# Last expert's rows placed by TensorE, x loaded and turned first, constants on SP's queue, key blocks reordered

## The chip, the cores and the metric
One core of one Trainium2 chip. The metric is the device time in microseconds of one execution, over several runs of each kernel.

## The reference
One layer of a diffusion backbone on 128 context tokens (condition c_ctx) and 512 latent tokens (condition c), width 1024, all in f32:

```
sh1, sc1, gt1, sh2, sc2, gt2 = silu(cond) @ w_ada + b_ada
h = rms_norm(x) * g_pre * (1 + sc1) + sh1 ;  p = h @ w_in
A: 8 heads, 2 kv heads, normed q/k, all latent keys and 128 cached keys
B: 8 heads, 2 kv heads, window of +-128, 128 cached keys, a sink logit
x = x + gt1 * rms_norm(concat(A, B) @ w_out) * g_post
h = modulate(x, sh2, sc2); aff = softmax(h @ w_router); 16 experts take their top 64 (latent), 16 (context) tokens
y_e = (silu(h_e @ w_gate) * (h_e @ w_up)) @ w_down * g ; summed onto the tokens
out = x + gt2 * rms_norm(sum) * g_post_ffn
```
Context tokens attend to context tokens only. The keys and values of the context are outputs too.

## The kernel before, in words
Tokens lie in TILES = 5 tiles of 128 (tile 0 context, 1 to 4 latent). Each engine has its own instruction stream; order is set by hand with semaphores. SP issues the large loads in the order of UNITS (the loop at L334): units of 2 MB into six slots of a ring, first ada(0) and ada(1) (w_ada's columns for shift and scale, two units each, 4 KB rows), the five tiles of x ahead of unit 2, the first unit of w_in (keys and values, two DMAs of 1 KB rows), its second unit, and then w_ada units whose slots come free when ada(0) and ada(1) are done.

Start. ACT issues six early loads (identity, gains, b_ada spread onto 32 rows a quarter: L801 to L806) and 17 loads of constants through `load` (L797). After them it computes silu of the condition (L826), the squares of x (L830) and, with the root from POOL, x normalised (L833). PE runs ada(0), turns its columns (mod_columns, L448), turns two of eight column blocks of x (turn_x, L464), runs ada(1), and then in project(0) turns a block, has it modulated by DVE (L1062) and ACT (L839) on the way out of PSUM, and multiplies the block before (L485). project(i) goes through 3 units of w_in times 5 tiles; ada(2) to ada(5) lie between (ADA_AFTER: ada(2) after project(2)). turn_qk (L502) turns the split q and k. POOL zeroes the DRAM sums sum_l, sum_c after project(0) (L1425).

Attention. 80 units (group, head, tile); group A first. Per unit u PE turns the probabilities of u - 1 (L546), computes the scores of u + 2 (L534), and every second unit multiplies with the values (L568). DVE takes the maximum (L1190) and scales (L1258), ACT does exp (L910) and copies the turned probabilities (L953). Cached keys lie at key columns 0 to 127, latent ones behind. key_parts gives the score matmuls of a unit: A 512 and 128 columns, B the cached keys and the window; each part is done twice (high and low part of the key). In B, w_out is multiplied beside it (L615).

Experts. Per expert 12 MB of weights pass through the ring; product_l (L721) and product_c (L733) use four column groups of PE at a time. turn_rows(e + 1) (L699, L701) turns the gathered rows of the next expert. DVE's weigh (L1376, L1377) scales the result, POOL's loop adds it in DRAM with two indirect DMAs (L1475, L1477).

End. When the last scatter has landed, SP reads the sums (L411), ACT squares them (L1013), DVE and POOL form mean and root and gate them (L1389, L1391, L1485), DVE adds x1 (L1399), ACT issues the stores (L1018).

## Time and profile before

| | us |
|---|---|
| median of 3 runs | 1024.57 (1022.05 to 1025.99) |
| the profiled execution, its own time | 1026.47 |
| its span | 1024.6 |
| PE busy | 911.5 (89%) |
| DVE, ACT, POOL busy | 335.3, 208.5, 138.9 |
| DMA | 269.03 MB, 263 GB/s mean |
| mean granted TensorE clock | 0.956 |

PE, PEld, DVE, ACT, POOL and SP are the engines, PE's weight loads being PEld; SPq, ACTq and POOLq rows are issues of DMAs. A matmul in f32 leaves two records. The span runs from the first to the last instruction or transfer.

### The profile page before, as it was taken

The page shows a single profiled execution, that of the slowest core. Times are in us where ns is not written, and L with a number is a line of the kernel's source. Part 1 is how long each engine was busy: PE and PEld are TensorE (multiplying, and loading weights), DVE is VectorE, ACT ScalarE, POOL GpSimd, SP SyncE. Part 2 cuts the span into 40 slices and gives each one's busy share as a digit, 9 for nine tenths or more (in the row PEclk, how much of TensorE's full clock was granted, in tenths as well). Part 3 has the DMA queues.
Part 4 walks back from the last instruction along what each step waited for, and adds up shares of the span by engine and source line. Part 5 has one row for each costly group of instructions (what it writes and reads, how often), then busy time and mean ns, then how long its engine had stood idle before and what let it go on. Part 6 is the DMA issues. An engine that isn't in the chain of part 4 may idle for free.

```text
span 1024.6 us, 20086 instructions
## 1 busy us (share of the span) xinstructions
PE 911.5 (89%) x8615; PEld 458.3 (45%) x8615; DVE 335.3 (33%) x880; ACT 208.5 (20%) x487; POOL 138.9 (14%) x213
## 2 busy tenths in 40 slices
PE   0399999899999999648999999999999999999970
PEld 0145555477776655443444444444444443444420
DVE  0045453587786774461011101111011100111015
ACT  0412221366664543030000000000000000000002
POOL 0110110000000000012022210222022210222034
PEclk9989999989999999668999999999999999999995
DMA  9976630220000004956999999999999999999735
GB/s 316 366 271 230 243 143 26 94 107 2 1 2 1 21 21 150 370 214 218 382 383 393 393 410 394 393 394 397 406 393 393 393 410 393 393 393 395 290 99 212
DMA packets 79101, 269.03 MB, mean 263 GB/s; under 512 B 6512, under 2 KB 13040, under 8 KB 79056
## 3 DMA queue, kind: packets, MB, share of 16 engines
q1 hardware_dynamic: 64816, 244.99, 61.6%
q0 software_dynamic: 7632, 16.13, 6.3%
q10 hardware_dynamic: 6608, 7.29, 2.1%
q8 instruction: 31, 0.51, 0.2%
q14 instruction: 14, 0.11, 0.0%
HBM read 253.84 MB, written 14.55 MB: 262 GB/s over the span
## 4 chain that ended last, share of the span: by engine, by line
PE 52%; DVE 2%; DMA 1%; issue 1%; ACT 1%; DVEq 0%; POOL 0%; SPq 0%; POOLq 0%; ACTq 0%
PE ps L721 32%; PE ps L733 17%; PE ps L699 1%; PE ps L767 1%; PE ps L762 1%; DMA reg_qt<-sum_l 0%; DMA sum_c<-reg,kt 0%; DVE reg_qt L1391 0%; PE ps L701 0%; PE ps L638 0%; DVE reg_qt L1399 0%; DMA reg<-rows_c,kt 0%; ACT reg L983 0%; DVE kt L1302 0%; DVEq L106 0%
## 5 line engine op out<-in xcount | busy, mean ns | idle before, releaser
L721 PE MATMUL ps<-ring,reg 128*32 128x512 f32 x2048 | 231.4, 592 | 0.0
L733 PE MATMUL ps<-ring,reg 128*32 128x256 f32 x2048 | 124.2, 384 | 3.2 <-DVE reg L1361 2.2
L721 PEld LDWEIGHTS ps<-ring,reg 128*32 128x32 f32 x2048 | 66.5, 110 | 126.2 <-issue 115.2
L1376 DVE TENSOR_SCALAR reg<-ps,kt 128x512 f32<-128x512 f32 x16 | 12.0, 751 | 330.3 <-PE ps L721 330.3
L485 PE MATMUL ps<-ring,reg_qt 128*128 128x512 f32 x240 | 106.5, 594 | 0.0
L733 PEld LDWEIGHTS ps<-ring,reg 128*32 128x32 f32 x2048 | 65.1, 111 | 68.6 <-issue 31.6
L1000 ACT ACTIVATE reg<-ps 128x256 f32<-128x256 f32 x16 | 6.1, 383 | 405.1 <-PE ps L762 405.1
L1419 POOL TENSOR_TENSOR small<-small,mhalf 128x1 f32<-128x1 f32 (+2 forms) x30 | 26.2, 876 | 396.2 <-DVE small L1208 246.1
L615 PE MATMUL ps<-ring,reg 128*128 128x512 f32 x160 | 78.6, 621 | 0.0
L485 PEld LDWEIGHTS ps<-ring,reg_qt 128*128 128x128 f32 x240 | 44.1, 190 | 50.0 <-issue 50.0
L437 PE MATMUL ps<-ring,reg 128*32 128x256 f32 x384 | 27.0, 444 | 41.0 <-ACT reg L826 41.0
L953 ACT ACTIVATE ring<-ps 128x640 f32<-128x640 f32 (+3 forms) x80 | 44.3, 553 | 71.5 <-PE ps L546 69.3
L721 PE MATMUL ps<-reg_qt,kt 128*32 128x512 f32 x512 | 57.9, 592 | 0.0
L721 PE MATMUL ps<-ring,kt 128*32 128x512 f32 x512 | 57.9, 592 | 0.0
L1190 DVE TENSOR_REDUCE small<-ps 128x1 f32<-128x640 f32 (+3 forms) x80 | 50.9, 636 | 15.0 <-PE ps L534 13.8
L546 PE MATMUL ps<-ident,ring 128*128 128x128 f32 x288 | 47.8, 284 | 6.1 <-ACT ring L953 4.0
L1446 POOL TENSOR_TENSOR small<-mhalf 128x1 f32<-128x1 f32 x34 | 6.5, 191 | 336.6 <-DVE reg L1377 335.1
L910 ACT ACTIVATE ring<-ps,small 128x640 f32<-128x640 f32 (+3 forms) x80 | 50.9, 636 | 0.7 <-DVE small L1195 0.7
L546 PEld LDWEIGHTS ps<-ident,ring 128*128 128x128 f32 x288 | 33.1, 142 | 28.5 <-issue 18.4
L615 PEld LDWEIGHTS ps<-ring,reg 128*128 128x128 f32 x160 | 29.0, 196 | 26.2 <-issue 26.2
L1258 DVE TENSOR_SCALAR ring<-ring,small 128x640 f32<-128x640 f32 (+3 forms) x80 | 36.8, 460 | 2.8
L437 PEld LDWEIGHTS ps<-ring,reg 128*32 128x32 f32 x384 | 13.5, 127 | 52.7 <-ACT reg L826 41.0
(177 smaller groups left out, 983.6 us busy)
## 6 DMA issues: line engine op xcount, KB each, us to landing
ring<-in_w_up SPq DMA_DIRECT2D x32, 2048.0 KB, 17.4
ring<-in_w_down SPq DMA_DIRECT2D x32, 2048.0 KB
ring<-in_w_gate SPq DMA_DIRECT2D x16, 2048.0 KB, 14.8
reg_qt<-in_w_gate SPq DMA_DIRECT2D x16, 2048.0 KB, 15.6
ring<-in_w_ada SPq DMA_DIRECT2D x12, 2048.0 KB, 10.9
reg<-in_x_sample SPq DMA_DIRECT2D x8, 512.0 KB, 13.6
ring<-in_w_in SPq DMA_DIRECT2D x2, 2048.0 KB, 17.0
ring<-in_w_out SPq DMA_DIRECT2D x2, 2048.0 KB
```

Source lines behind the costliest of these rows:

```text
L437: last = pe.matmul(ps[32 * q:32 * q + 32, 4, 0:QUART], silu[:, 4 * h + c, :], w[:, c, q * QUART:(q + 1) * QUART], start=(h == 0 and c == 0 ...
L485: last = pe.matmul(ps[:, i % 2, :], hT[:, c, t * P:(t + 1) * P], w[:, c, :], start=(c == 0), stop=(c == KC - 1))
L546: last = pe.transpose(two[2][:, b * P:(b + 1) * P], probs[:, u % 3, b * P:(b + 1) * P], ident[:, :])
L615: last = pe.matmul(out_at(o)[:, n, :], attnT[:, c, t * P:(t + 1) * P], unit_at(wout_units[c // 4], 4)[:, c % 4, n * 512:(n + 1) * 512], st ...
L721: last = pe.matmul(o[64 * n + r:64 * n + r + 32, :], x[:, j, hf, r:r + 32], w[:, j, n * HALF:(n + 1) * HALF], start=(hf == 0 and j == 0), ...
L733: last = pe.matmul(o[32 * q:32 * q + 32, :], x[:, c % 2, c // 2, :], w[:, j, q * QUART:(q + 1) * QUART], start=(c == 0), stop=(c == KC - 1))
L910: act.activation(probs[:, u % 3, 0:n], scores_at(u)[:, 0:n], ACT.Exp, bias=negm[:, b:b + 1], scale=DH ** -0.5, accum_out=den[:, b:b + 1]). ...
L953: act.activation(pT[:, k % 2, u % 2, 0:n], two[2][:, 0:n], ACT.Copy).then_inc(pT_ready, 1)
L1190: link(dve.tensor_reduce(mx[:, b:b + 1], scores_at(u)[:, 0:n], AX.X, ALU.max))
L1258: dve.tensor_scalar(probs[:, u % 3, 0:n], probs[:, u % 3, 0:n], rden[:, b:b + 1], None, ALU.mult)\
L1376: dve.tensor_scalar(y_l, ps[:, 3, :], g_l[:, bass.ds(e, 1)], None, ALU.mult)
L1419: pool.tensor_tensor(dst, mean, mhalf[:, 0:n], ALU.pow).then_inc(done, 1)
```

## The change
- Start: x is loaded ahead of all weights; b_ada goes to the two used rows of each quarter of a buffer that DVE has cleared. The constants are issued by SP, seven of them (keys, gains, rope) behind the first w_in unit and waited for as keys_in, ten behind the second as consts_in. The first w_in unit comes in two halves of K. PE turns all eight blocks of x before ada(0); they are copied out unmodulated and modulated in place afterwards.
- Attention: the cached keys lie between latent blocks 1 and 2, so that a window is one stretch of columns. A's scores are 320 + 320 columns, B's one part.
- Last expert: no turn_rows, no weigh, no scatter. POOL numbers the columns, DVE builds from them matrices that hold the gate at (row, its token) and PE multiplies them with the copied result: context sums and tile 1 are added to the loaded sums by DVE, for tiles 2 to 4 PE adds the loaded sum with an identity matmul. Squares and gating read PSUM. SP waits for the sums of the other 15 experts, reads them, and issues the stores. POOL gathers no rows past the last expert.

```diff
...
-POOL_GATED = (0, 2)
+SUM_BANKS = {1: 6, 2: 0, 3: 2, 4: 4}
+SUMMED_BY_PE = (2, 3, 4)
...
+KEY_AT = {-1: 2 * P, 0: 0, 1: P, 2: 3 * P, 3: 4 * P}
+WINDOWS = {1: [0, 1, -1], 2: [0, 1, -1, 2], 3: [1, -1, 2, 3], 4: [-1, 2, 3]}
...
+def value_blocks(g, t):
+    if t == 0:
+        return [4]
+    return [0, 1, -1, 2, 3] if g == 0 else WINDOWS[t]
...
 def key_parts(g, t):
     if t == 0:
         return [(0, TOK, CTX)]
+    first, n = KEY_AT[value_blocks(g, t)[0]], key_count(g, t)
     if g == 0:
-        return [(0, 0, 512), (512, 512, TOK - 512)]
-    lo, hi = max(0, t - 2), min(LT - 1, t)
-    return [(0, 0, CTX), (CTX, CTX + lo * P, (hi + 1 - lo) * P)]
...
+        return [(0, first, n // 2), (512, first + n // 2, n // 2)]
+    return [(0, first, n)]
...
+            def load_keys():
+                for n, name in enumerate(("cache_a_k", "cache_a_v", "cache_b_k", "cache_b_v")):
+                    sp.dma_start(cache[:, n * P:(n + 1) * P], A[name][0, 0].rearrange("t h d -> t (h d)")).then_inc(keys_in, 16)
+                for n, name in enumerate(("g_qa", "g_ka")):
+                    sp.dma_start(gqk[:, n * DH:(n + 1) * DH], A[name].to_broadcast([P, DH])).then_inc(keys_in, 16)
+                sp.dma_start(rope[:, :, :, :].rearrange("p a t d -> p (a t) d"),
+                             A["rope_tables"].rearrange("a (t p) d -> p (a t) d", p=P)).then_inc(keys_in, 16)
+            def load_consts():
+                sp.dma_start(sink[:, :], A["sink_b"].to_broadcast([P, HEADS])).then_inc(consts_in, 16)
+                sp.dma_start(wr[:, :].rearrange("p (c e) -> p c e", e=E),
+                             A["w_router"][0].rearrange("(c p) e -> p c e", p=P)).then_inc(consts_in, 16)
+                for n, name in enumerate(("g_post_attn", "g_post_ffn")):
+                    rows = A[name].rearrange("a (q n) -> q a n", q=4)
+                    for q in range(4):
+                        sp.dma_start(gpost[32 * q:32 * q + 32, n * QUART:(n + 1) * QUART],
+                                     rows[q].to_broadcast([32, QUART])).then_inc(consts_in, 16)
...
-                if u == 2:
+                if u == 0:
...
                     if m == 0:
-                        sp.dma_start(d[:, :, 0:256], w[:, :, 512:768]).then_inc(slot_in[slot_of(u)], 16)
-                        sp.dma_start(d[:, :, 256:512], w[:, :, 1280:1536]).then_inc(slot_in[slot_of(u)], 16)
+                        for b in (0, 1):
+                            k = slice(4 * b, 4 * b + 4)
+                            sp.dma_start(d[:, k, 0:256], w[:, k, 512:768]).then_inc(win0_in[b], 16)
+                            sp.dma_start(d[:, k, 256:512], w[:, k, 1280:1536]).then_inc(win0_in[b], 16)
+                        load_keys()
...
+                        if m == 1:
+                            load_consts()
...
-            sp.wait_ge(added_l, 16 * (E + 1))
-            sp.wait_ge(added_c, 16 * (E + 1))
+            sp.wait_ge(added_l, 16 * E)
+            sp.wait_ge(added_c, 16 * E)
+            sp.wait_ge(gate_b, E)
...
+            for t in range(TILES):
+                sp.wait_ge(f_ready, t + 1)
+                dst = out[0][0] if t == 0 else out[1][0, (t - 1) * P:t * P]
+                sp.dma_start(dst, gated[:, t, :]).then_inc(stored, 16)
+            sp.wait_ge(stored, 16 * (4 + TILES))
...
-            pe.wait_ge(silu_ready, 1)
-            ada(0)
             pe.wait_ge(early_in, 16 * N_EARLY)
-            mod_columns(0, 0)
...
-                    pe.wait_ge(ht_ready, c - 1)
-                    pe.wait_ge(htc_ready, c - 1)
+                    pe.wait_ge(ht_raw, c - 1)
+                    pe.wait_ge(htc_raw, c - 1)
...
-            turn_x(0)
-            turn_x(1)
+            for c in range(KC):
+                turn_x(c)
+            pe.wait_ge(silu_ready, 1)
+            ada(0)
+            mod_columns(0, 0)
             ada(1)
             mod_columns(1, 1)
...
                 for c in range(KC):
                     if i == 0:
-                        if c + 2 < KC:
-                            turn_x(c + 2)
                         pe.wait_ge(htc_ready, c + 1)
+                        if c % 4 == 0:
+                            pe.wait_ge(win0_in[c // 4], 32)
...
-                turn_rows(e + 1)
+                if not final:
+                    turn_rows(e + 1)
...
+                if final:
+                    weight_in(5, e)
+                    product_c(5, YC[:, 0:QUART], aT_c).then_inc(down_c, 1)
+                    pe.wait_ge(actT_l_ready, e + 1)
+                    product_l(4, Y, aT_l).then_inc(down_a, 1)
+                    product_l(5, Y, aT_l).then_inc(down_b, 1)
+                    return
...
+            def total_onto(t, n):
+                pe.wait_ge(sum_in[t], 16)
+                pe.matmul(sums_at(t)[:, n, :], ident[:, :], total[:, t, n * HALF:(n + 1) * HALF], start=True, stop=False)
+            def last_onto(t):
+                for n in (0, 1):
+                    last = pe.matmul(sums_at(t)[:, n, :], put_on_l[64 * n:64 * n + 64, (t - 1) * P:t * P],
+                                     y_l[64 * n:64 * n + 64, :], start=t not in SUMMED_BY_PE, stop=True)
+                last.then_inc(put_on, 1)
+            pe.wait_ge(put_on_ready, 1)
+            pe.wait_ge(y_copied_c, 1)
+            pe.wait_ge(silu_done, 2 * E)
+            pe.wait_ge(actT_l_ready, E)
+            for q in range(4):
+                last = pe.matmul(ps[:, (0, 1, 2, 5)[q], 0:QUART], put_on_c[32 * q:32 * q + 32, :],
+                                 y_c[32 * q:32 * q + 32, :], start=True, stop=True)
+            last.then_inc(put_on, 1)
+            pe.wait_ge(f_added, 1)
+            total_onto(2, 0)
+            pe.wait_ge(y_copied_l, 1)
+            last_onto(1)
+            total_onto(2, 1)
+            last_onto(2)
+            for t in (3, 4):
+                total_onto(t, 0)
+                total_onto(t, 1)
+                last_onto(t)
...
+            act.wait_ge(bias_cleared, 1)
             for q in range(4):
-                act.dma_start(modq[32 * q:32 * q + 32, :, :], b_rows[q:q + 1].to_broadcast([32, N_MOD, QUART]))\
+                act.dma_start(modq[32 * q:32 * q + 2, :, :], b_rows[q:q + 1].to_broadcast([2, N_MOD, QUART]))\
...
+            for c in range(KC):
+                act.wait_ge(xt_done, c + 1)
+                act.activation(hT[:, c, 0:P], ps[:, 5 + c % 2, 0:P], ACT.Copy).then_inc(htc_raw, 1)
...
             act.wait_ge(modcol_ready, 2)
             for c in range(KC):
-                act.wait_ge(xt_done, c + 1)
-                act.activation(hT[:, c, 0:P], ps[:, 5 + c % 2, 0:P], ACT.Identity, bias=cmod[:, 0, 0, c:c + 1],
+                act.wait_ge(htc_raw, c + 1)
+                act.activation(hT[:, c, 0:P], hT[:, c, 0:P], ACT.Identity, bias=cmod[:, 0, 0, c:c + 1],
                                scale=cmod[:, 1, 0, c:c + 1]).then_inc(htc_ready, 1)
...
-                    act.wait_ge(consts_in, 16 * N_CONSTS)
+                    act.wait_ge(keys_in, 16 * N_KEYS)
...
-                act.activation(probs[:, u % 3, 0:n], scores_at(u)[:, 0:n], ACT.Exp, bias=negm[:, b:b + 1],
+                dst = probs[:, u % 3, 0:n]
+                if g == 0 and t:
+                    dst = dst.rearrange("p (b n) -> p b n", b=2)
+                act.activation(dst, scores_of(u), ACT.Exp, bias=negm[:, b:b + 1],
                                scale=DH ** -0.5, accum_out=den[:, b:b + 1]).then_inc(exp_done, 1)
...
-            for t in range(TILES):
-                act.wait_ge(sum_in[t], 16)
-                act.activation(squares[:, t, :], total[:, t, :], ACT.Square,
+            act.wait_ge(added_l, 16 * E)
+            act.wait_ge(added_c, 16 * E)
+            act.wait_ge(down_c, 1)
+            act.activation(y_c, ps[:, 4, 0:QUART], ACT.Copy).then_inc(y_copied_c, 1)
+            def square_sum(t):
+                if t in SUMMED_BY_PE:
+                    act.wait_ge(put_on, t + 1)
+                    if t < TILES - 1:
+                        act.wait_ge(f_gated, t + 1)
+                    src = sums_at(t)
+                else:
+                    act.wait_ge(f_added, t + 1)
+                    src = total[:, t, :].rearrange("p (a n) -> p a n", a=2)
+                act.activation(squares[:, t, :].rearrange("p (a n) -> p a n", a=2), src, ACT.Square, scale=1.0 / 32.0,
                                accum_out=ssf[:, t:t + 1]).then_inc(f_squared, 1)
-            for t in range(TILES):
-                act.wait_ge(f_ready, t + 1)
-                dst = out[0][0] if t == 0 else out[1][0, (t - 1) * P:t * P]
-                act.dma_start(dst, total[:, t, :]).then_inc(stored, 16)
-            act.wait_ge(stored, 16 * (4 + TILES))
+            square_sum(0)
+            act.wait_ge(down_b, E)
+            act.activation(y_l, ps[:, 3, :], ACT.Copy).then_inc(y_copied_l, 1)
+            for t in range(1, TILES):
+                square_sum(t)
...
+            dve.memset(mod[:, :], 0.0).then_inc(bias_cleared, 1)
...
+            for c in range(KC):
+                dve.wait_ge(xt_done, c + 1)
+                dve.tensor_copy(hT[:, c, P:TOK], ps[:, 2 + c % 2, :]).then_inc(ht_raw, 1)
...
+                dve.wait_ge(ht_raw, c + 1)
+                dve.tensor_scalar(hT[:, c, P:TOK], hT[:, c, P:TOK], cmod[:, 1, 1, c:c + 1], cmod[:, 0, 1, c:c + 1],
                                   ALU.mult, ALU.add).then_inc(ht_ready, 1)
...
+            dve.wait_ge(consts_in, 16 * N_CONSTS)
+            link(dve.tensor_scalar(nsink[:, :], sink[:, :], -1.0, None, ALU.mult))
...
-                link(dve.tensor_reduce(mx[:, b:b + 1], scores_at(u)[:, 0:n], AX.X, ALU.max))
+                        m = 0 if before else 1
+                        link(dve.tensor_tensor(scores_at(u)[:, P:2 * P], scores_at(u)[:, P:2 * P], masks[:, m, :], ALU.add))
+                if g == 0 and t:
+                    link(dve.tensor_reduce(mx[:, b:b + 1], scores_of(u), AX.XY, ALU.max))
+                else:
+                    link(dve.tensor_reduce(mx[:, b:b + 1], scores_of(u), AX.X, ALU.max))
...
+            modulate(E - 1, 1)
+            activations(E - 2)
+            weigh(E - 2)
+            dve.tensor_copy(last_row_l, row_l[:, E - 1:E])
+            dve.tensor_copy(last_row_c, row_c[:, E - 1:E]).then_inc(last_rows, 1)
+            dve.wait_ge(last_rows, 1)
+            dve.wait_ge(numbered, 6)
+            dve.wait_ge(gate_b, E)
+            dve.tensor_scalar(put_on_l, number_l, last_row_l, g_l[:, E - 1:E], ALU.is_equal, ALU.mult)
+            dve.tensor_scalar(put_on_c, number_c, last_row_c, g_c[:, E - 1:E], ALU.is_equal, ALU.mult)\
+                .then_inc(put_on_ready, 1)
+            activations(E - 1)
...
+            def gate_sum(t):
+                if t in SUMMED_BY_PE:
+                    dve.wait_ge(put_on, t + 1)
+                    if t == TILES - 1:
+                        dve.wait_ge(f_squared, TILES)
+                    src = sums_at(t)
+                else:
+                    src = total[:, t, :].rearrange("p (a n) -> p a n", a=2)
+                dve.tensor_tensor(gated[:, t, :].rearrange("p (a n) -> p a n", a=2), src,
+                                  gate_rows[:, min(t, 1), :].rearrange("p (a n) -> p a n", a=2), ALU.mult)\
+                    .then_inc(f_gated, 1)
+            def add_x1(t):
                 dve.wait_ge(f_rstd, t + 1)
...
+                dve.wait_ge(f_gated, t + 1)
+                dve.scalar_tensor_tensor(gated[:, t, :], gated[:, t, :], rsf[:, t:t + 1], xr[:, t, :],
                                          ALU.mult, ALU.add).then_inc(f_ready, 1)
...
+            dve.wait_ge(up_b, E)
+            dve.wait_ge(sum_in[0], 16)
+            dve.wait_ge(put_on, 1)
+            quarters = total[:, 0, :].rearrange("p (q n) -> p q n", q=4)
+            dve.tensor_tensor(quarters[:, 0:3], quarters[:, 0:3], ps[:, 0:3, 0:QUART], ALU.add)
+            dve.tensor_tensor(quarters[:, 3], quarters[:, 3], ps[:, 5, 0:QUART], ALU.add).then_inc(f_added, 1)
+            dve.wait_ge(f_added, 1)
+            gate_sum(0)
+            add_x1(0)
+            dve.wait_ge(sum_in[1], 16)
+            dve.wait_ge(put_on, 2)
+            halves = total[:, 1, :].rearrange("p (a n) -> p a n", a=2)
+            dve.tensor_tensor(halves, halves, sums_at(1), ALU.add).then_inc(f_added, 1)
+            dve.wait_ge(f_added, 2)
+            gate_sum(1)
+            gate_sum(2)
+            add_x1(1)
+            gate_sum(3)
+            add_x1(2)
+            add_x1(3)
+            gate_sum(4)
+            add_x1(4)
...
-            with pool.Fori(0, E) as e:
-                pool.wait_ge(xe_turned, e + 2)
-                gather(e + 2)
...
+            with pool.Fori(0, E - 2) as e:
+                pool.wait_ge(xe_turned, e + 2)
+                gather(e + 2)
+                scatter(e)
+            scatter(E - 2)
+            pool.wait_ge(gate_b, E - 1)
+            pool.wait_ge(held_ops, 2 * E - 1)
+            for h in (0, 1):
+                pool.iota(number_l[64 * h:64 * h + 64, :], [[2, LAT]], base=h, channel_multiplier=0,
+                          allow_small_or_imprecise_dtypes=True).then_inc(numbered, 1)
+            for q in range(4):
+                pool.wait_ge(numbered, 2 + q)
+                pool.iota(number_c[32 * q:32 * q + 32, :], [[4, CTX]], base=q, channel_multiplier=0,
+                          allow_small_or_imprecise_dtypes=True).then_inc(numbered, 1)
             for t in range(TILES):
+                pool.wait_ge(f_squared, t + 1)
+                pool.tensor_scalar(msf[:, t:t + 1], ssf[:, t:t + 1], EPS, None, ALU.add).then_inc(f_mean, 1)
                 root(rsf[:, t:t + 1], msf[:, t:t + 1], 1, f_mean, f_rstd, t + 1)
-                if t in POOL_GATED:
-                    pool.wait_ge(f_squared, t + 1)
-                    pool.tensor_tensor(total[:, t, :], total[:, t, :], gate_rows[:, min(t, 1), :], ALU.mult)\
-                        .then_inc(f_gated_pool, 1)
...
```

## Rows read from the trace of the kernel before

**Rows 1.** The page: busy tenths of PE in 40 slices.
```profile
PE   0399999899999999648999999999999999999970
```

**Rows 2.** Windows: start and length, busy us of PE, PEld, DVE, ACT, POOL, clock, DMA share, GB/s.
```profile
0.00:40.00 40.00, 0.00 (x0) 0.00 (x0) 0.34 (x2) 0.54 (x1) 0.50 (x5) 1.00 0.98 336
0.00:55.00 55.00, 11.59 (x96) 5.76 (x100) 1.78 (x10) 11.89 (x17) 3.26 (x10) 0.96 1.01 345
480.00:960.00 480.00, 480.00 (x5788) 198.05 (x5784) 64.11 (x118) 27.55 (x60) 89.50 (x147) 1.00 1.03 393
```

**Rows 3.** Timeline, ACT's queue and ACT: start, us, engine, line, operation, count, [idle before].
```profile
12.95 11.92 ACTq L797 DMA_DIRECT2D sink<-in_sink_b  x1
...
39.46 1.28 ACT L826 ACT_TABLE_LOAD   x1 [39.46 <-issue]
...
45.03 1.04 ACT L830 ACTIVATE reg_qt<-reg 128x1024 f32<-128x1024 f32 x1
...
46.07 5.29 ACT L833 ACTIVATE reg<-reg,small 128x1024 f32<-128x1024 f32 x5
```

**Rows 4.** Timeline, PE and DVE from 41 to 87 us.
```profile
41.02 6.60 PE L437 MATMUL ps<-ring,reg 128*32 128x256 f32 x64 [41.02 <-ACT reg L826]
...
52.89 5.79 PE L437 MATMUL ps<-ring,reg 128*32 128x256 f32 x64
...
67.31 0.81 DVE L1062 TENSOR_SCALAR reg_qt<-ps,colmod 128x512 f32<-128x512 f32 x1 [0.60 <-PE ps L464]
...
68.51 7.03 PE L485 MATMUL ps<-ring,reg_qt 128*128 128x512 f32 x16
...
86.66 3.66 PE L437 MATMUL ps<-ring,reg 128*32 128x256 f32 x64
```

**Rows 5.** Windows in ada(1), and while POOL's zeroing moves.
```profile
52.00:54.00 2.00, 2.00 (x17) 1.16 (x19) 0.00 (x0) 0.00 (x0) 0.00 (x0) 0.50 1.03 412
...
75.00:85.00 10.00, 10.00 (x31) 4.93 (x30) 5.06 (x19) 1.86 (x5) 0.79 (x2) 1.00 0.79 229
```

**Rows 6.** Timeline, a pair of units of group A; the last row from the lines.
```profile
253.17 0.74 PE L546 MATMUL ps<-ident,ring 128*128 128x128 f32 x5 [0.25 <-ACT ring L953]
253.85 0.90 PE L534 MATMUL ps<-k_a,q_a 128*128 128x512 f32 x4
...
253.94 0.70 ACT L953 ACTIVATE ring<-ps 128x640 f32<-128x640 f32 x1
...
254.54 0.79 ACT L910 ACTIVATE ring<-ps,small 128x640 f32<-128x640 f32 x1
...
L924 ACT ACTIVATE reg_qt<-ps 128x1024 f32<-128x1024 f32 x4 | 4.1, 1020 | 0.0
```

**Rows 7.** Timeline, last expert and end.
```profile
974.71 0.65 PE L699 MATMUL ps<-ident,reg 128*128 128x128 f32 x4
...
989.18 3.62 PE L721 MATMUL ps<-ring,reg 128*32 128x512 f32 x32
...
1001.46 0.34 SPq L411 DMA_DIRECT2D reg_qt<-sum_c  x1
...
1005.28 1.06 ACT L1013 ACTIVATE reg<-reg_qt 128x1024 f32<-128x1024 f32 x1 [22.30 <-DMA reg_qt<-sum_c]
1006.24 0.19 ACT L1013 ACTIVATION_READ_ACCUMULATOR reg<-reg_qt 128x1 f32 x1
...
1017.62 3.66 DVE L1399 SCALAR_TENSOR_TENSOR reg_qt<-reg_qt,small,reg 128x1024 f32<-128x1024 f32 x3
```

**Rows 8.** Prices: page group, IOTA, root on POOL, and a DVE pass over PSUM.
```profile
L721 PE MATMUL ps<-ring,reg 128*32 128x512 f32 x2048 | 231.4, 592 | 0.0
...
436.38 0.19 POOL L1439 IOTA kt<- 16x64 f32 x1
...
1006.79 0.57 POOL L1419 TENSOR_TENSOR small<-small,mhalf 128x1 f32<-128x1 f32 x1 [8.15 <-DVE small L1389]
...
L1215 DVE SCALAR_TENSOR_TENSOR reg_qt<-ps,small,reg_qt 128x1024 f32<-128x1024 f32 x3 | 3.8, 1278 | 0.2 <-POOL small L1419 0.2
```

More of the change, by code:

```diff
@@ L308, in build @@
         N_EARLY = 6
-        N_CONSTS = 17
-        LOADS = [sum((2 if UNITS[v][:2] == ("win", 0) else 1) for v in range(len(UNITS)) if slot_of(v) == s)
-                 for s in range(SLOTS)]
+        N_KEYS = 7
+        N_CONSTS = 10
+        LOADS = [sum(UNITS[v][:2] != ("win", 0) for v in range(len(UNITS)) if slot_of(v) == s) for s in range(SLOTS)]
         block = ctx.enter_context(nc.Block())
@@ L416, in landed @@
             def landed(u):
-                loads = sum((2 if UNITS[v][:2] == ("win", 0) else 1) for v in range(u + 1) if slot_of(v) == slot_of(u))
+                loads = sum(UNITS[v][:2] != ("win", 0) for v in range(u + 1) if slot_of(v) == slot_of(u))
                 pe.wait_ge(slot_in[slot_of(u)], 16 * loads)
@@ L474, in project @@
                     pe.wait_ge(ht_ready, KC)
-                if t == 0:
+                if t == 0 and s:
                     landed(win_units[s])
@@ L745, in gate_product, with expert @@
                 product_l(s, G, xT_l[odd]).then_inc((gate_a, gate_b)[half], 1)
[L747 removed]
+            def expert(e, odd, following, final=False):
                 weight_in(2, e)
@@ L1379, in _ @@
             modulate(0, 0)
-            with dve.Fori(0, E // 2) as pair:
+            with dve.Fori(0, E // 2 - 1) as pair:
                 for odd in (0, 1):
```

90 lines of the change are left out of this document (30 added, 60 removed).

## The prediction

> **What bounds the kernel now.** I read the slices of the page first. The reader is to see PE at 9 in nearly all of them, but at 0 in the first slice and in most of the second, at 6 and 4 around 410 to 460 us, and at 0 in the last [rows 1]. Then the windows: from 480 to 960 us PE is busy all 480 us, so the expert loop is bound by TensorE and can only be shifted; in the first 40 us PE does nothing while the DMA engines are 0.98 busy [rows 2]. The timeline of the start says why. ACT issues 23 loads, one of them holding it for 11.92 us, and its first computing instruction is a table load at 39.46 us; the squares of x, the normalised x and ada(0) all wait for it [rows 3, 4]. So 41 us pass before PE starts, by when ada's first weights and x are long there. At the other end PE is done at 992.8 (989.18 + 3.62), and 31.8 us follow without it: weigh, two scatters, reading the sums back, norm, gate, store [rows 7].
>
> **Start: x first, constants off ACT.** This is the largest term. ACT keeps six small issues and reaches its silu at about 7 us, so it is no longer what comes last; next are the DMAs. Bytes in the new order: small things 0.13 MB, x 2.62, ada(0) 4.19, ada(1) 4.19, the first w_in unit 2.10. The same engines moved 336 GB/s over the first 40 us, 13.4 MB [rows 2]. So x is in by 8 (2.75/0.336) to 11 us, ada(0) by about 22, ada(1) (11.1 MB) by 33, w_in (13.2 MB) by 39.5.
> ACT squares the tiles as they come (1.04 us each) and normalises all five in 5.29 us [rows 3]: to 18 us. Eight turn_x rounds follow. A round was limited before by a DVE evacuation of 0.81 us between turns, and had a projection matmul in it; I take 0.9 to 1.4 us a round: to 25 to 29 us. ada(0) costs 3.66 us as at 86.66, or 6.60 us as at 41.02, where its pitch is that of the half rate [rows 4]: to 29 to 35 us, and some 1.3 us to turn its columns. ada(1) then has its weights; it ends at 35 to 40 us, and 1.3 us later the first block is modulated.
> The evacuation is now a plain copy before the modulation is known, and the modulation is a second pass in SBUF: eight more instructions on DVE and on ACT. Before, PE went through project(0) in steps of turn, modulate, multiply; now the passes (at most 0.81 us each) keep ahead of the 0.88 us of a matmul. project(0) takes 7.03 us for its 16 records at the full rate [rows 4] and has its first half of w_in before 39.5: it ends at 46.5 to 50, I take 47. Before it ended at 71.1 (six of the 16 records from 68.51 on are its own).
> Not all of these 24 us arrive. ada(2) started at 86.66 [rows 4]. PE would now come to it at 47 + 2 projections of 7.03 + 2 turns of 0.9 = 63. By then 20.5 MB must be in: 19.0 of them by 55 us at the rate of 0 to 55 [rows 2], the rest by 59. But the zeroing of the sums, which POOL issues when project(0) is done, now falls into this very stretch. Alone with one weight unit it filled 0.79 of 10 us [rows 5]. It can delay ada(2) by nothing or by 7 us, so its weights land at 59 to 66. I take 64 for its start, 1 us of waiting: **22.5 us gained**, from 16.5 (PE at 70 by a cold start and full delay) to 25.
> SP is moved past too: it issues seven key loads behind the first w_in unit and ten constants behind the second. In front of ada(2) these are 0.9 MB and about 3000 small packets, counted in the 20.5 MB; w_in's second unit is wanted only after project(4), some 30 us later, and hides all of its delay. DVE and ACT wait for the keys only (by about 43 us), and what stands behind that wait, the rope products and the first high part, has until project(0) ends.
> The Trainium skill ("DMA: Bandwidth & Descriptors", Queues, rings and completion order) says that each DMA engine takes turns between the queues that have work, a packet at a time. By it the zeroing does get its turns inside ada(2)'s load; the overlap itself no run shows yet, and the bounds above stand without it.
>
> **Attention: key blocks reordered.** Group A's scores become 320 + 320 columns in place of 512 + 128; group B's context and window blocks lie side by side, so four instructions become two. Five transposes of 128 columns take 0.74 us with the tail of the last, so a narrow instruction costs about 0.11 us of PE time. In A, scores take 0.90 us, and PE then waits 0.25 us for ACT's copy of the turned probabilities, which takes 0.70 us and does not depend on the scores [rows 6]; a faster score matmul gives nothing there. In B, PE is the fuller engine in 32 wide units: 32 x 0.11 = 3.5 us at most. I take 1.5, from -2 (reading two banks in one access costs a little) to 3.5.
>
> **Tail: last rows by PE.** First the last expert. It no longer turns the rows of an expert that does not exist: 0.65 us and its surroundings, 1.2 us in all [rows 7]. Against it, DVE builds the placing matrices ahead of this expert's activations, and waits for six iotas on POOL. An iota of 64 columns is 0.19 us [rows 8]; of 512, by size, 0.7 to 2, so all six take 3 to 5 us from about 975.6, over by 978.5 to 981. DVE was to start on the activations at 977 to 978.2, so they lose 0.5 to 3 us. Nearly all else there is the same. PE ends its last product at T0 = 991.8, between 991.5 and 994. The sum of the other experts is scattered by 981.5 and read back in 3.8 us (1001.46 to 1005.28 before [rows 7]), now beside 10 us of PE work: hidden.
> From T0, with a matmul of 128x512 at 0.88 us, a DVE pass over 1024 columns at 1.28 us from PSUM and 1.22 us from SBUF, an ACT square at 1.25 us with its accumulator read, and 0.8 us for POOL's mean and root (0.57 the root alone) [rows 4, 7, 8]: four context products to +1.8; added on DVE +3.2; ACT squares it to +4.5 and only then copies y_l, to +5.1. PE puts tile 1 on by +6.9, tile 2 by +9.5, tile 3 by +13.0, tile 4 by +16.6 (two identity and two placing matmuls each, 3.5 us). For tile 4 ACT squares to +17.9, DVE gates to +19.2 and adds to +20.5. DVE's own work is 15.5 us, so PE sets this end. The last store went 3.3 us from DVE's end (1021.28) to the end of the span: T0 + 23.8 = 1015.6. Against 1024.6 this is 9.0; PE's matmuls may partly overlap, which I count at 0.5: **9.5 us gained**. Bounds: the DVE sum alone, T0 + 19.5 (a gain of 13.5), and a loss of clock after PE's gaps, as at the start, where the granted clock was 0.50 from 52 to 54 us (1.2 GHz, after a stretch in which PE had waited on ACT) and ada(1) took 5.79 us in place of 3.66 [rows 4, 5]; some 3 us, with a late T0: T0 + 27 from 994 (a gain of 4).
>
> **How the numbers follow.** 22.5 + 1.5 + 9.5 = 33.5 us. The profiled execution was 1026.47 us (span 1024.6, 1.9 around it), so 993.0; it was itself 1.9 above the median of the runs, of which I take off half: **992 us**.
>
> **Rivals.** (a) *Placing matmuls run side by side.* They use 32 or 64 rows of the array each and write different banks. The nearest row is for columns: 32 records of L721, each 592 ns, in 3.62 us [rows 7, 8]. If rows do the same, the four context products take 0.5 us and each pair 0.88 us; then DVE sets the end at T0 + 21.5, 2.3 us earlier: 990. Against it: no matmul of before is split by rows. The Trainium skill ("TensorE: Matmul & The Clock Gate", Part 3: Packing small matmuls — row/col tiling) says that tiles on different row groups do run concurrently.
> (b) *The DMAs set the start after all.* Small packets on SP's ring, the zeroing and 1 KB rows of w_in add up, ada(2) starts at 70 or later: the gain is 16 or less, 998 to 1003. For it: DMA share 0.98 in the first 40 us [rows 2].
> (c) *The start doesn't move*, because something of ACT's queue still holds the silu or x: 1026.5 - 11 = 1015. Against it: of 23 loads ACT keeps six, the first and small ones, ahead of the 11.92 us one [rows 3].
> (d) *Slower.* Exp and maximum in group A now read two pieces of 320 columns in two banks. If such an access ran at half speed, each of 32 units would lose the 0.79 us of its exp [rows 6] and as much for its maximum, 1.6 us in all, 51 us: 1043. It decides from 1.05 us a unit. Against it: L924 reads 2 x 512 columns of two banks in 1.02 us, 1 ns a column [rows 6].
>
> Chances: forecast 0.47, (a) 0.28, (b) 0.14, (c) 0.05, (d) 0.02, and 0.04 for anything below 980. The range takes in (a), most of (b) and the bounds of the start: 980 to 1003. This kernel's measurement can tell about 0.5% (5 us) from no change. Faster by more: 0.96; within: 0.02, the worst of (c); slower: 0.02, that is (d).
>
> **What would show each step.** ACT's table load before 10 us; turn_x before ada(0); project(0) over at 46 to 50; ada(2) starting at 62 to 66 with at most 3 us of waiting on its weights; group A's pair of units still at 4.4 us; the expert loop unchanged at 480 us for the same stretch; no scatter after PE's last product; five stores of which the last ends 23 to 25 us behind it. The forecast is wrong if PE waits for w_ada or w_in for over 5 us after project(0), if ada(0) waits for x, or if the iotas hold DVE beyond 981.

## The result and the profile after

The changed kernel takes 990.72 us (median of four runs, 990.34 to 996.82) against 1023.88 us (1022.05 to 1025.99) of the kernel before in the same comparison: a ratio of 0.969, with a 95% interval of 0.965 to 0.973. The profiled execution took 990.57 us, its span is 988.8 us.

The page of the kernel after: PE's busy tenths, to be held against [rows 1], and the totals.

```profile
span 988.8 us, 20026 instructions
PE 915.3 (93%) x8581; PEld 451.5 (46%) x8581; DVE 336.1 (34%) x887; ACT 211.5 (21%) x497; POOL 125.5 (13%) x207
...
PE   3879999899999999459999999999999999999995
```

PE is as busy as before (915.3 us against 911.5), so what went is idle time: the empty first slice is a 3 now, the empty last one a 5. The dip that began around 410 us before (6, 4, 8) is still there, some 20 us earlier (4, 5, 9).

The start of the kernel after in its timeline: the queues of ACT and SP, then ACT (start, us, engine, line, operation, count; [rows 3] answers to them).

```profile
4.24 1.28 ACT L897 ACT_TABLE_LOAD   x1 [4.24 <-issue]
...
12.42 1.06 ACT L901 ACTIVATE reg_qt<-reg 128x1024 f32<-128x1024 f32 x1 [0.60 <-DMA reg<-in_x_sample]
...
13.48 5.29 ACT L904 ACTIVATE reg<-reg,small 128x1024 f32<-128x1024 f32 x5
```
```profile
30.77 2.06 SPq L346 DMA_DIRECT2D cache<-in_cache_a_k  x1
...
38.27 2.41 SPq L354 DMA_DIRECT2D sink<-in_sink_b  x1
...
41.20 5.99 SPq L360 DMA_DIRECT2D gpost<-in_g_post_attn  x4
47.23 5.46 SPq L360 DMA_DIRECT2D gpost<-in_g_post_ffn  x4
52.73 19.44 SPq L387 DMA_DIRECT2D ring<-in_w_ada  x5
```

ACT's first computing instruction is at 4.24 us instead of 39.46, and it now waits for x tile by tile (0.6 us before the last). The constants take issuing time on SP too: the ten from the sink on take it from 38.27 to 52.69 us, 14.4 us (before, ACT was at them from 12.95 us to its table load at 39.46 [rows 3]). SP does nothing else then, and ada(2)'s weights are issued behind them.

PE and POOL's queue in the same stretch ([rows 4] answers to it):

```profile
14.75 0.45 PE L514 MATMUL ps<-ident,reg 128*128 128x128 f32 x1 [14.75 <-ACT reg L904]
...
25.67 3.66 PE L490 MATMUL ps<-ring,reg 128*32 128x256 f32 x64
...
36.73 14.00 PE L538 MATMUL ps<-ring,reg_qt 128*128 128x512 f32 x32 [0.86 <-ACT reg_qt L915]
...
58.31 1.04 PE L555 MATMUL ps<-ident,reg 128*128 128x128 f32 x8
63.08 1.93 PE L490 MATMUL ps<-ring,reg 128*32 128x256 f32 x32 [3.73 <-DMA ring<-in_w_ada]
68.31 3.43 PE L490 MATMUL ps<-ring,reg 128*32 128x256 f32 x32 [3.30 <-DMA ring<-in_w_ada]
```
```profile
44.18 1.39 POOL L1561 DMA_DIRECT2D sum_l<-reg_qt  x1 [29.80 <-PE ps L538]
```

The x32 row holds project(0) and project(1): the first is over at 43.8 us (ACT copies its context part at 43.90), where it was over at 71.1. ada(2) is over at 71.7 instead of 90.3, 8.7 us less of a gain. The two bracketed waits of 3.73 and 3.30 us, for its own weights, are 7.0 us of this. Another 1.5 us come behind the second wait: the second half takes 3.43 us where the first takes 1.93, at a mean granted clock of 0.55. The windows show this, and what the DMA engines did meanwhile (start and length, busy us of PE, PEld, DVE, ACT, POOL, clock, DMA share, GB/s; kernel after).

```profile
36.00:41.00 5.00, 4.27 (x10) 2.01 (x11) 3.88 (x10) 3.19 (x8) 0.00 (x0) 1.00 0.65 168
...
60.00:65.00 5.00, 1.92 (x32) 1.13 (x32) 3.92 (x15) 0.37 (x1) 0.07 (x1) 1.00 1.01 396
...
68.31:71.74 3.43, 3.43 (x33) 1.47 (x33) 0.00 (x0) 0.00 (x0) 0.00 (x0) 0.55 1.02 413
```
```profile
0.00:68.30 68.30, 41.45 (x268) 22.63 (x268) 24.94 (x82) 22.83 (x47) 8.16 (x16) 1.00 0.97 349
```

They were full but for the first 4 us and one hole at 36 to 41 us, just behind the issues of the seven small key loads (30.77 to 35.70 us). Over the 68.3 us until the last weights of ada(2) were used they moved 349 GB/s: 23.8 MB.

The tail of the kernel after, from PE's last product (967.45 = 960.40 + 7.05) on, some rows of each engine:

```profile
950.08 1.79 POOL L1623 IOTA ring<- 64x512 f32 x2
951.94 1.13 POOL L1627 IOTA ring<- 32x128 f32 x4
```
```profile
960.40 7.05 PE L775 MATMUL ps<-ring,reg 128*32 128x512 f32 x64
...
967.38 0.71 PE L869 MATMUL ps<-reg,ring 32*128 32x256 f32 x8
968.26 0.96 DVE L1526 TENSOR_TENSOR reg_qt<-reg_qt,ps 128x768 f32<-128x768 f32 x1 [11.98 <-PE ps L869]
...
971.27 1.13 PE L860 MATMUL ps<-reg,ring 64*128 64x512 f32 x4 [0.54 <-ACT reg L1111]
971.77 1.28 DVE L1519 SCALAR_TENSOR_TENSOR ring<-ring,small,reg 128x1024 f32<-128x1024 f32 x1 [0.96 <-POOL small L1555]
```
```profile
979.33 1.13 PE L860 MATMUL ps<-reg,ring 64*128 64x512 f32 x4
...
981.11 1.28 DVE L1519 SCALAR_TENSOR_TENSOR ring<-ring,small,reg 128x1024 f32<-128x1024 f32 x1 [1.01 <-POOL small L1555]
...
983.63 1.28 DVE L1519 SCALAR_TENSOR_TENSOR ring<-ring,small,reg 128x1024 f32<-128x1024 f32 x1
```

From PE's last product to the end it is 21.35 us, against 31.8 us before [rows 7]. The whole account, by the same instruction in both traces:

| up to | before | after | gained so far | in this stretch |
|---|---|---|---|---|
| ada(2) over | 90.3 | 71.7 | 18.6 | 18.6 |
| first matmul of the router | 406.0 | 383.9 | 22.1 | 3.5 |
| affinities turned (L676, now L730) | 427.5 | 402.0 | 25.4 | 3.3 |
| last expert's first L762, now L817 | 953.1 | 928.7 | 24.4 | -1.0 |
| last product over | 992.8 | 967.45 | 25.35 | 0.95 |
| end of the span | 1024.6 | 988.8 | 35.8 | 10.4 |

The 3.3 us at the router are no instruction that the change takes away: PE's granted clock differs over the same instructions. The router's stretch in windows, before and then after:

```profile
406.00:427.50 21.50, 19.91 (x90) 14.47 (x89) 3.86 (x9) 1.54 (x4) 0.00 (x0) 0.76 0.90 347
```
```profile
383.90:402.00 18.10, 16.55 (x89) 12.02 (x87) 3.85 (x9) 1.53 (x4) 0.00 (x0) 0.91 1.01 393
```

Of the two levels (1.2 and 2.4 GHz) PE had the lower one for 10.2 us of this stretch before and for 3.4 us after. At the first expert it went the other way, the -1.0: a clock of 0.85 over its first 20 us before, 0.81 after.

### The profile page after: what moved, and what is told of

It reads as the page before. It is cut to its first block, busy times and chain, and to the rows that moved or that the text cites. A ratio compares the mean times of both kernels' runs of the same rounds, so it can differ in the third digit from the quotient of the medians.

```text
span 988.8 us, 20026 instructions
## 1 busy us (share of the span) xinstructions
PE 915.3 (93%) x8581; PEld 451.5 (46%) x8581; DVE 336.1 (34%) x887; ACT 211.5 (21%) x497; POOL 125.5 (13%) x207
## 4 chain that ended last, share of the span: by engine, by line
PE 54%; DVE 2%; ACT 1%; issue 1%; POOL 0%; DMA 0%; DVEq 0%; ACTq 0%
PE ps L775 33%; PE ps L787 17%; PE ps L753 1%; PE ps L822 1%; PE ps L817 1%; DVE ring L1512 0%; PE ps L755 0%; DVE ring L1519 0%; PE ps L692 0%; ACT reg L1064 0%; DMA reg<-rows_c,kt 0%; ACT ring L1106 0%; DVE kt L1406 0%; DVE kt L1405 0%; DVE reg_qt L1534 0%
## 5 line engine op out<-in xcount | busy, mean ns | idle before, releaser
L787 PE MATMUL ps<-ring,reg 128*32 128x256 f32 x2048 | 124.2, 384 | 3.2 <-DVE reg L1465 2.2
L775 PEld LDWEIGHTS ps<-ring,reg 128*32 128x32 f32 x2048 | 66.7, 110 | 127.4 <-issue 116.8
L787 PEld LDWEIGHTS ps<-ring,reg 128*32 128x32 f32 x2048 | 65.1, 111 | 68.2 <-issue 31.0
L1555 POOL TENSOR_TENSOR small<-small,mhalf 128x1 f32<-128x1 f32 (+2 forms) x30 | 23.0, 766 | 357.9 <-DVE small L1312 239.3
L599 PEld LDWEIGHTS ps<-ident,ring 128*128 128x128 f32 x288 | 33.1, 142 | 32.4 <-issue 20.7
L587 PE MATMUL ps<-k_a,q_a 128*128 128x320 f32 (+1 forms) x144 | 33.2, 353 | 1.9 <-DVE q_b L1214 1.9
L621 PE MATMUL ps<-ring,v_lat 128*64 128x128 f32 x416 | 33.7, 279 | 0.0
L490 PE MATMUL ps<-ring,reg 128*32 128x256 f32 x384 | 23.9, 400 | 7.7 <-DMA ring<-in_w_ada 7.7
## 6 DMA issues: line engine op xcount, KB each, us to landing
ring<-in_w_down SPq DMA_DIRECT2D x32, 2048.0 KB, 16.5
ring<-in_w_in SPq DMA_DIRECT2D x2, 2048.0 KB, 10.4
ring<-in_w_out SPq DMA_DIRECT2D x2, 2048.0 KB, 10.4
```

Of the source, the lines that this page charges most:

```text
L490: last = pe.matmul(ps[32 * q:32 * q + 32, 4, 0:QUART], silu[:, 4 * h + c, :], w[:, c, q * QUART:(q + 1) * QUART], start=(h == 0 and c == 0 ...
L587: last = pe.matmul(scores_at(u)[:, at:at + n], qT[g][:, h, t * P:(t + 1) * P], kT[g][:, 2 * (h // 4) + part, k0:k0 + n], start=(part == 0) ...
L599: last = pe.transpose(two[2][:, b * P:(b + 1) * P], probs[:, u % 3, b * P:(b + 1) * P], ident[:, :])
L621: last = pe.matmul(ps[64 * hh:64 * hh + 64, bank, 0:P], v, pT[:, k % 2, hh, n * P:(n + 1) * P], start=(n == 0), stop=(n == len(blocks) - 1))
L775: last = pe.matmul(o[64 * n + r:64 * n + r + 32, :], x[:, j, hf, r:r + 32], w[:, j, n * HALF:(n + 1) * HALF], start=(hf == 0 and j == 0), ...
L787: last = pe.matmul(o[32 * q:32 * q + 32, :], x[:, c % 2, c // 2, :], w[:, j, q * QUART:(q + 1) * QUART], start=(c == 0), stop=(c == KC - 1))
```

## The experiments

The theory behind them: three independent gains, of which the start's comes from ACT's queue alone, and ada(2)'s 7.0 us of waiting come from bytes and issues put ahead of its weights. The rival: x's place, or the order of SP's issues, is what counts.

**The three parts alone.** Each of the first three kernels is the kernel before with one part of the change: its start, its key blocks, its tail. A line or two of each, of the start:

```diff
-            pe.wait_ge(silu_ready, 1)
-            ada(0)
+            for c in range(KC):
+                turn_x(c)
```

of the key blocks:

```diff
-        return [(0, 0, 512), (512, 512, TOK - 512)]
+        return [(0, first, n // 2), (512, first + n // 2, n // 2)]
```

and of the tail:

```diff
-            sp.wait_ge(added_l, 16 * (E + 1))
+            sp.wait_ge(added_l, 16 * E)
```

> The kernel before with the start of the change alone (x first and turned first, constants on SP, w_in in halves); keys and tail as before. Theory: the three parts add up, and the start gives 18.6 us (project(0) over at 44 instead of 71, of which 7 us are lost again in waits for w_ada in ada(2)): 1023.9 - 18.6 = 1005, with ada(2) over at 71.5 to 72.5. Rival: the parts don't add up, since the earlier start lets something else come last in attention or routing: 1010 or more.

> The kernel before with the reordered keys alone. Theory: scores of group A 1.2 us and of group B 2.3 us shorter from their first to their last, as read from the trace of the changed kernel: 1020.4. Rival: reading two banks in one access costs in exp and maximum what the matmuls give, and the 3.5 us seen are of the clock: 1023 to 1025.

> The kernel before with the last expert and the end of the change alone. Theory: 0.95 us before the last product and 10.4 us after it (21.4 instead of 31.8): 1012.5, and the stretch from PE's last product of the experts to the end of the span 21.4 us. Rival: part of the 10.4 us belongs to the clock or to other parts: 1015 or more.

Measured against 1023.45 us in the same comparison: the start alone 1005.32 us (ratio 0.9811, interval 0.9787 to 0.9836), the key blocks alone 1020.53 (0.9974, 0.9959 to 0.9989), the tail alone 1013.13 (0.9898, 0.9879 to 0.9917). The gains are 18.1, 2.9 and 10.3 us, 31.3 together; all at once gave 33.2 (1023.88 - 990.72). With the tail alone it is 21.3 us from PE's last product (over at 990.09) to the end of the span, as expected. So the parts add; the 1.9 us left over are within what the intervals of four numbers allow, and of the size of the clock's part above. The kernel with the start alone has PE wait for the same two units, 6.1 us in place of 7.0, and both halves of ada(2) run at the lower clock in it (3.64 us each, granted clock 0.50). From its timeline:

```profile
63.80 3.64 PE L475 MATMUL ps<-ring,reg 128*32 128x256 f32 x32 [4.76 <-DMA ring<-in_w_ada]
68.78 3.64 PE L475 MATMUL ps<-ring,reg 128*32 128x256 f32 x32 [1.34 <-DMA ring<-in_w_ada]
```

**Constants back on ACT's queue.** The changed kernel, in which ACT issues the 17 loads behind its own six:

```diff
-                        load_keys()
...
-                        if m == 1:
-                            load_consts()
...
+            load_keys()
+            load_consts()
+
             act.wait_ge(cond_in, 16)
```

> The changed kernel with the 17 constants issued by ACT again, behind its six early loads; all else as changed, x first too. Theory: ACT's issues are what held the start. Its table load comes at 30 to 39 us again, turn_x after 43, and the kernel loses most of the 27 us of project(0): project(0) over at 62 to 71 and the time 1008 to 1016. Rival: with x in front ACT's queue is free sooner, since SP's ring is what slowed it: table load below 20 us, time within 5 us of 990.7.

One run: 1011.35 us. ACT's queue and first instruction in it:

```profile
8.06 9.21 ACTq L883 DMA_DIRECT2D sink<-in_sink_b  x1
...
18.64 14.13 ACTq L889 DMA_DIRECT2D gpost<-in_g_post_attn  x4
...
34.80 1.28 ACT L897 ACT_TABLE_LOAD   x1 [34.80 <-issue]
```

Some 21 of the 33 us are gone, with x still first and turned first: project(0) is over at 71.0 us and ada(2) starts at 86.56, as in the kernel before (71.1 and 86.66). That leaves about 12 us, which is what key blocks and tail give alone (13.2): the whole gain of the start hangs on ACT's queue. What moving the loads alone would give, with all else of the start as before, was not run. The row to see is the sink again: 4 KB of data, and the engine that issues it stands for 9.21 us, here as before (11.92 us [rows 3]), while SP's loads keep the DMA engines full (a share of 0.98 from 8.0 to 17.3 us).

**x third again.** The changed kernel, with x loaded ahead of unit 2:

```diff
-                if u == 0:
+                if u == 2:
                     for t in range(TILES):
```

> The changed kernel with x loaded behind ada(0)'s two units, as before the change; all else as changed. Theory: x comes 4.2 MB or 12 us later, turn_x is over at 38 instead of 26, project(0) at about 55 instead of 43.8; ada(2) then doesn't wait, so that of the 11 to 12 us the 7 us of waits come back: 994 to 996. Rival: the order of x is worth nothing since w_ada and w_in bound the start: 990 to 992.

One run: 992.49 us; my theory of 994 to 996 missed, and the time is half a us above the rival's range; in its trace the router's stretch takes 19.9 us, 1.8 more than in the changed kernel's. So x's place is worth nothing here, as the rival had it, though not for its reason, that the weights bound the start: here PE does not wait for them. project(0) starts at 45.49 us instead of 36.73, but PE comes to ada(2) at 68.04 and does not wait:

```profile
45.49 14.00 PE L538 MATMUL ps<-ring,reg_qt 128*128 128x512 f32 x32 [0.86 <-ACT reg_qt L915]
...
68.04 3.66 PE L490 MATMUL ps<-ring,reg 128*32 128x256 f32 x64
```

It is over at 71.70 us, as in the changed kernel (71.74). The 8.8 us that x first gives PE are all spent again there: 7.0 in waiting for w_ada and 1.5 in the second half at the lower clock.

**What ada(2) waits for.** Three kernels: the zeroing of the sums issued by POOL two projections later, at 59 us instead of 44.18; the ten constants issued behind the third w_in unit instead of the second; and both.

```diff
-            pool.wait_ge(proj_done, 1)
-            pool.wait_ge(zeros_set, 1)
-            pool.dma_start(sum_l.rearrange("(p a) (b n) -> p (a b) n", p=P, n=QUART),
...
+                if i == 2:
+                    pool.wait_ge(zeros_set, 1)
+                    pool.dma_start(sum_l.rearrange("(p a) (b n) -> p (a b) n", p=P, n=QUART),
```
```diff
-                        if m == 1:
+                        if m == 2:
                             load_consts()
```

> The changed kernel with the three zeroing DMAs of POOL issued behind the root of project(2) and not of project(0), some 15 us later. In the changed kernel PE waits 3.7 and 3.3 us for the two units of ada(2). Theory: the zeroing (2.8 MB, 7 to 8 us of DMA time) lay ahead of and among these units; without it they land 5 to 7 us earlier, the waits fall to 0 to 2 us and the time to 984 to 986. Rival: the constants on SP's ring are what delays them, and the zeroing shares only leftovers: waits of over 5 us, 989 to 991.

> The changed kernel with the ten constants issued behind the third unit of w_in (about 87 us) and not behind the second. SP spent 14.4 us on issuing them, from 38.3 to 52.7 us, and issued ada(2)'s units only then. Theory (the DMA engines were busy all the time, so only bytes and packets count): 0.33 MB and 1400 packets are 2 to 3 us, waits fall from 7 to 4 or 5 us, 988. Rival (SP's queue was held by its issues, and the units came late because they were issued late): the waits vanish, 984.

> Both moves together. Theory: 7.0 us of waits for w_ada is all that there is to gain; PE comes to ada(2) at 59.4 us and has its weights: 983.5 to 984.5, not less than with the zeroing late alone by over 2 us. Rival: the start is bound by DMA further on (ada(3) then waits): 986 or more.

| | us | interval of the ratio | ada(2) over | PE's waits on w_ada | router's stretch |
|---|---|---|---|---|---|
| the change | 990.72 | 0.965 to 0.973 | 71.7 | 7.7 | 18.1 |
| zeroing late | 984.77 | 0.960 to 0.964 | 64.0 | 2.0 | 19.9 |
| constants late | 989.60 | 0.964 to 0.969 | 66.7 | 4.8 | 21.5 |
| both late | 981.42 | 0.957 to 0.960 | 62.1 | 0.8 | 18.2 |

(Waits with those of 0.7 to 1.0 us inside ada(1). The router's stretch goes from its first matmul to the turned affinities, in the one trace of each kernel.) ada(2) in the kernel with the zeroing late, then with the constants late, then with both:

```profile
58.95 1.93 PE L490 MATMUL ps<-ring,reg 128*32 128x256 f32 x32
62.07 1.93 PE L490 MATMUL ps<-ring,reg 128*32 128x256 f32 x32 [1.18 <-DMA ring<-in_w_ada]
```
```profile
58.48 1.93 PE L490 MATMUL ps<-ring,reg 128*32 128x256 f32 x32
64.27 2.40 PE L490 MATMUL ps<-ring,reg 128*32 128x256 f32 x32 [3.86 <-DMA ring<-in_w_ada]
```
```profile
58.42 3.66 PE L490 MATMUL ps<-ring,reg 128*32 128x256 f32 x64
```

It looks mostly like bytes. The zeroing moves 2.75 MB, 7.9 us at 349 GB/s; without it the second half starts at 62.07 instead of 68.31, 6.2 us earlier. The two causes are not wholly apart in this kernel, since SP also issued ada(2)'s weights 4.6 us earlier (48.16 instead of 52.73). But issuing alone is not it. The constants are few bytes in many packets: taking them away and issuing ada(2)'s weights 15 us earlier (37.63 instead of 52.73) gives only 4.0 us (64.27 instead of 68.31), some of which may be run to run: the same start in the kernel with another order in the tail, below, had the second half at 66.75.

As a time, 989.60 is not told apart from 990.72, and the traces say why: the kernel with the constants late is 3.6 us ahead at the first matmul of the router (380.3 instead of 383.9), and the router's stretch at a lower clock takes 3.4 us of this back.

With both away nothing is left to wait for in ada(2), and the kernel with both is the fastest start. It came out 2 to 3 us below its expectation, and 3.4 below the zeroing late alone, where at most 2 were expected. 1.9 us of this are at ada(2); part of the rest is the clock. In its trace PE had the lower level for 3.4 us of the router's stretch, with the zeroing late alone for 6.8. And in the tail of that latter trace the clock was 0.55 from 964.2 to 968.0 us, so that 22.8 us passed behind its last product instead of 21.3.

**x third, with both moved.** Does x first pay once nothing waits?

> Both moves at the start, but x loaded ahead of unit 2 again, as before the change. With x third the changed kernel came to ada(2) at 68.0 us and found its weights there; with x first it was over with ada(2) at the same time, because it waited 7 us for them. Theory (x first is worth its 9 to 10 us only once the waits are gone): ada(2) starts at 67.5 to 68.5 us in place of 58.4, and the time is 981.4 + 9.6 = 991. Rival (x's place in the queue never matters, the constants' and the zeroing's places were all of it): ada(2) starts by 62 and the time stays below 985.

Two runs: 993.11 us, 11.7 above the kernel with both moved. ada(2) starts at 67.23 us without a wait, 8.8 later than the 58.42 above. So x's place is worth 9 us there, as the theory had it, and nothing in the change as it stands. The rest arises at the router, whose stretch (its first matmul to the turned affinities) takes 21.4 us in this trace and 18.2 in that of the kernel with both moved: the clock again, by 3 us.

**Another order in the tail.** PE adds tile 1's loaded sum too, and DVE and ACT take tile 1 earlier:

```diff
-SUMMED_BY_PE = (2, 3, 4)
+SUMMED_BY_PE = (1, 2, 3, 4)
...
-            square_sum(0)
             act.wait_ge(down_b, E)
             act.activation(y_l, ps[:, 3, :], ACT.Copy).then_inc(y_copied_l, 1)
+            square_sum(0)
...
             gate_sum(0)
-            add_x1(0)
-            dve.wait_ge(sum_in[1], 16)
-            dve.wait_ge(put_on, 2)
-            halves = total[:, 1, :].rearrange("p (a n) -> p a n", a=2)
-            dve.tensor_tensor(halves, halves, sums_at(1), ALU.add).then_inc(f_added, 1)
-            dve.wait_ge(f_added, 2)
             gate_sum(1)
+            add_x1(0)
```

> The changed kernel with a tail in another order: PE adds the loaded sum of tile 1 too (identity matmuls ahead of the placing ones), so DVE loses its 1.3 us addition for that tile; ACT copies the last latent result before it squares tile 0; DVE gates tile 1 before it adds x1 to tile 0. Theory (behind PE's last product DVE's own work and its two waits of 1.0 us for a root set the end, not PE): one DVE pass of 1.3 us goes and half of the waits with it, PE to the end falls from 21.35 to 19.4 us, 988.8 in all. Rival 1 (PE sets it, since each placing pair waits for the copy): PE gets two matmuls more, 1.8 us, and tail and total stay where they are, 990.5 to 991.5. Rival 2 (DVE waits for roots as much as it works less): 20.7 us or more behind PE's last product, 990.

> Both moves at the start (zeroing behind ada(2)'s wait, the ten constants behind the third w_in unit) together with the tail in the other order. Theory: start and tail share nothing, so the 1.9 us of the tail come off the 981.4 of the kernel with both moves: 979.5, and PE to the end takes 19.4 us. Rival: the tail's order gives nothing (PE or roots set it): 981 to 982.

989.84 us and 980.98 us. From the last product to the end it takes 20.7 us in both (987.3 - 966.63; 979.4 - 958.7), 0.7 less than 21.35, not 1.9. The time fits the second rival, but the mechanism is the first one's. From the timeline of the first of these kernels:

```profile
973.15 1.99 PE L855 MATMUL ps<-reg_qt,ident 128*128 128x512 f32 x4
973.27 1.23 DVE L1511 TENSOR_TENSOR ring<-ps,reg_qt 128x1024 f32<-128x1024 f32 x1 [0.56 <-PE ps L860]
...
975.06 1.13 PE L860 MATMUL ps<-reg,ring 64*128 64x512 f32 x4
...
976.12 1.98 PE L855 MATMUL ps<-reg_qt,ident 128*128 128x512 f32 x4
976.24 1.23 DVE L1511 TENSOR_TENSOR ring<-ps,reg_qt 128x1024 f32<-128x1024 f32 x1 [0.56 <-PE ps L860]
```

A tile costs PE 2.97 us (1.98 for the sum, 1.13 to place, from one to the next), DVE 2.5 us; DVE's gating now waits 0.56 us for PE in the last two. The work taken off DVE was put on the engine that was nearly as late. The version with both moves at the start and this tail is, at 980.98 us (0.957 to 0.962), the lowest of all, but not told apart from 981.42.

## Why the prediction was right, and where it was not

The total was: 992 against 990.7. Step by step:

- *Cause of the start.* Right. ACT's silu at 5.5 us, turn_x before ada(0), ada(0) at the full rate (3.66 us), project(0) over at 43.8, ahead of the 46.5 to 50: turn_x began at 14.75 us and its eight rounds took 11 us, so that all of this came a little earlier than I had it.
- *ada(2) at 64 with 1 us of waiting, 22.5 us gained.* This failed, and the text had named 5 us of waiting for w_ada as what would prove it wrong; it was 7.0, in two pieces, at halves that the prediction did not look at. 3.7 us of the 7 are only PE coming at 59.35 us and not at 63. The gain was 18.6, inside 16.5 to 25, since ada(2) was over at 71.7 and not 67.7. Two terms were mis-sized. One is when the weights are in. The bytes and their rate were right: 23.8 MB had moved by 68.3 us, of which 2.75 are the zeroing. But I had all of ada(2) in by 59 us without the zeroing, and 62.07 is what PE found in the kernel with the zeroing late. Of the 0 to 7 us of delay by the zeroing my 64 took 5; it cost 6.2 measured and 7.9 by its bytes. The other is the clock, at nothing in this term: behind the wait of 3.30 us it fell, and the second half took 1.5 us more. The row that I held against a full delay, a share of 0.79 [rows 5], was of a stretch in which it had the engines nearly to itself and so could not say what it takes from others. The rule that I cited on turns between queues (the Trainium skill, "DMA: Bandwidth & Descriptors", Queues, rings and completion order) was the better guide: by it the zeroing gets its turns, and the runs agree, with the 6.2 us. Rival (b), the DMAs set the start, was so for ada(2) in its mechanism, though not in its size: ada(2) started at 63.08 and not at 70 or later, and its 998 to 1003 did not come.
- *SP moved past: hidden.* Half right. The second w_in unit was never waited for. But the ten issues put those of ada(2)'s weights back by 15 us, and without them ada(2) is over 5.0 us earlier (1.9 with the zeroing away too).
- *Attention 1.5.* 3.5 by the account, 2.9 as a part alone: the upper bound of 3.5. Group A's pair of units went from 4.40 to 4.36 us, as expected; from B's first unit to the router 2.3 us were gained, where I had scaled down the 3.5. The accesses over two banks cost nothing seen: the exp of 640 columns is 0.79 us in both [rows 6], so rival (d) falls.
- *Last expert.* Right: 0.95 us gained where 1.0 was taken (T0 from 992.8 to 991.8). The six iotas took 2.9 us (1.79 + 1.13), just under the 3 to 5, and were over 14 us ahead of PE's last product.
- *Tail 9.5.* Rival (a) was right: placing matmuls on different rows of the array run side by side. From the groups of the last 29 us of the kernel after (busy us, mean ns of one):

```profile
L860 PE MATMUL ps<-reg,ring 64*128 64x512 f32 x16 | 4.5, 641 | 0.5 <-ACT reg L1111 0.5
...
L869 PE MATMUL ps<-reg,ring 32*128 32x256 f32 x8 | 0.7, 426 | 0.0
```

Eight records of 426 ns in 0.71 us, and four of 641 ns in 1.13 us. I had 1.8 us for the first and 1.76 for the second, with 0.5 off for an overlap; rival (a) said 0.5 and 0.88. It gave T0 + 21.5; measured 21.35. The rule of the Trainium skill ("TensorE: Matmul & The Clock Gate", Part 3: Packing small matmuls — row/col tiling), named there beside it, is borne out by this trace. That DVE alone sets the end then, as the rival had it, is not quite so: the other tail order shows PE nearly as late.
- *What no step had.* 3.3 us at the router and -1.0 at the first expert, from the granted clock. They (+2.3), the attention (+2.0) and rival (a) (+1.9: 0.95 + 10.45 us at the last expert and the tail, where I had 9.5) made up for the 3.9 us missing at the start: 33.5 predicted, 35.8 by the spans. That the total was nearer than its terms is luck.

## What to carry to other kernels

An engine that computes should not issue loads while the queues are full: a 4 KB load held ACT for 9 to 12 us here, and with it and sixteen other loads back on ACT none of the 18 us at the start was left. When work is pulled forward, count every byte that is due before the next big load, including writes of another engine that the earlier finish itself triggers; at full DMA share the zeroing cost 6.2 us, near its bytes divided by the rate (7.9). Gains that arrive at a wait (x first here, worth 0 or 9 us) show only once that wait is gone, so try both orders again afterwards. And a wait of TensorE can cost more than its own length: 1.5 us of lower clock came behind the one of 3.30 us.

## What the runs showed of the hardware that I had not expected

- The time of an issue does not follow the size of the load: four gpost loads of 32 KB took ACT 14.13 us to issue in one kernel (its second four 1.91 us), and SP 5.99 and 5.46 us in another. What sets it no run here takes apart.
- Behind the seven small key loads on SP's queue there is a hole: at 36 to 41 us the DMA engines moved 168 GB/s, with 353 in the 6 us before and 369 in the 4 us behind. With the key loads on ACT's queue they moved 313 GB/s from 35 to 40 us. The hole is in the trace of the kernel with both moves as well (180 GB/s), which is some 2 to 3 us of DMA time that nothing uses yet.
- The granted clock at the router differs between kernels that are the same there: the lower level held for 3.4, 6.8 or 10.2 us of it, and the stretch took 18.1 to 18.2 us in four of the thirteen traces (the changed kernel among them), 19.9 in five and 21.4 to 21.5 in four (the kernel before among them). Each kernel has one trace, so whether the edit or the execution decides is open. A difference of 3 us between two traces must be looked for there before it is put down to an edit.
